# Queries and keys of the first block: projected by rows, turned in 16 columns a head, then transposed; the fifth conditioning chunk loaded ahead of the values'

## The reference, cut to what matters

```
c_act = silu(c)
mod   = c_act @ w_ada + b_ada                    # shift1, scale1, gate1, shift2, scale2, gate2
h     = rmsnorm(x) * norm_mix_g * (1 + scale1) + shift1
proj  = h @ w_in                                 # 512 pool | 512 q | 512 k | 512 v | 2048 gates
q, k  = rope_partial(q, pos), rope_partial(k, pos)   # 8 heads of 64
attn  = causal softmax attention over 256 tokens
merged = sigmoid(gates) * (pooled @ w_branch_pool) + ... attn @ w_branch_attn
x     = x + gate1 * (merged @ w_out)
x     = x + gate2 * peer_ffn(...)                # 256 rows of gathered experts a token tile
...then the second block: attention, convolution FFN

def rope_partial(x, pos):          # only 16 of a head's 64 columns turn
    x1, x2, rest = x[..., :8], x[..., 8:16], x[..., 16:]
    return concatenate([x1 * cos - x2 * sin, x1 * sin + x2 * cos, rest])
```

## Time and profile before

| | us |
|---|---|
| median of 3 runs | 1170.46 |
| lowest, highest | 1169.34, 1170.64 |
| the profiled execution | 1169.51 |
| its span in the profile | 1167.7 |
| its mean granted TensorE clock | 0.976 of full speed |

### The profile page before, as it was taken

The page is one execution under the profiler, slowest core; times in us unless marked ns, Lnnn a source line. Parts: engine busy times, 40 slices in busy tenths (PEclk is TensorE's granted clock), DMA queues, the critical chain, the costliest instruction groups (busy, mean ns, idle before and its releaser), DMA issues.

```text
span 1167.7 us, 13710 instructions
## 1 busy us (share of the span) xinstructions
PE 1037.7 (89%) x5050; PEld 698.5 (60%) x5050; DVE 824.5 (71%) x1912; ACT 420.8 (36%) x895; POOL 301.0 (26%) x262
## 2 busy tenths in 40 slices
PE   6989999989999896887877788788899999999997
PEld 3889976645555443432323333233389878999986
DVE  6599765867777767788878655555566878888843
ACT  3545622322332132132221211111266666565631
POOL 0000001444554553444544444445000000000000
PEclk9999999999999999988988999989999999999999
DMA  9977593999999999999999999999894443554530
GB/s 377 424 322 299 236 403 153 422 421 421 421 421 420 421 421 421 421 409 421 421 422 422 421 422 421 422 421 422 340 393 180 145 181 144 191 208 170 192 144 36
DMA packets 48342, 390.44 MB, mean 334 GB/s; under 512 B 5514, under 2 KB 5906, under 8 KB 7316
## 3 DMA queue, kind: packets, MB, share of 16 engines
q0 software_dynamic: 37040, 269.51, 55.6%
q1 hardware_dynamic: 11236, 120.07, 26.3%
HBM read 388.50 MB, written 1.06 MB: 334 GB/s over the span
## 4 chain that ended last, share of the span: by engine, by line
PE 51%; DMA 34%; DVE 11%; ACT 2%; issue 2%; POOL 1%; SPq 0%; DVEq 0%
DMA ring<-in_uv,idx 30%; PE ps L1466 18%; PE ps L1832 13%; PE ps L1989 5%; DMA ring<-in_w_ada 3%; DVE ring L1252 3%; PE ps L1700 2%; PE ps L1642 2%; PE ps L1917 2%; PE ps L1490 1%; DVE ring L904 1%; DVE ring_r L893 1%; PE ps L1715 1%; PE ps L1519 1%; ACT probT L765 1%
## 5 line engine op out<-in xcount | busy, mean ns | idle before, releaser
L1832 PE MATMUL ps<-ring,probT 128*128 128x512 f32 x1020 | 490.1, 624 | 102.0 <-ACT probT L765 101.9
L1252 DVE CUSTOM_DVE_ANT_0 ring<-h2t,ring 128x1024 f32<-128x1024 f32 x255 | 309.9, 1223 | 178.6 <-DMA ring<-in_uv,idx 178.3
L1832 PEld LDWEIGHTS ps<-ring,probT 128*128 128x128 f32 x1020 | 190.8, 198 | 337.7 <-issue 189.9
L522 POOL DMA_INDIRECT ring<-in_uv,idx x255 | 298.6, 1171 | 325.8 <-PE ps L1832 275.7
L1466 PE MATMUL ps<-util_r,ring_r 128*128 128x256 f32 x1216 | 204.6, 282 | 0.0
L893 DVE TENSOR_TENSOR ring_r<-ring,ring_r 128x1024 fp32r<-128x1024 f32 (+1 forms) x134 | 155.6, 1205 | 36.3 <-ACT ring_r L544 36.3
L1466 PEld LDWEIGHTS ps<-util_r,ring_r 128*128 128x128 f32 x1216 | 169.7, 188 | 0.8 <-issue 0.7
L760 ACT ACTIVATE prob<-prob 128x2 f32<-128x2 f32 (+2 forms) x98 | 20.0, 204 | 400.7 <-DVE prob L1252 400.5
L544 ACT ACTIVATE ring_r<-ring 128x1024 fp32r<-128x1024 f32 (+1 forms) x134 | 131.9, 1039 | 44.4 <-DMA ring<-in_w_in 22.0
L1466 PE MATMUL ps<-h_r,ring_r 128*128 128x256 f32 x704 | 125.2, 281 | 0.6 <-DVE util_r L1224 0.6
L765 ACT ACTIVATE probT<-ct,prob 128x128 f32<-128x128 f32 x256 | 85.5, 392 | 87.0 <-DVE prob L1258 86.4
(11 more groups left out here) (217 smaller groups left out, 995.5 us busy)
## 6 DMA issues: line engine op xcount, KB each, us to landing
ring<-in_w_in SPq DMA_DIRECT2D x11, 2048.0 KB, 12.4
ring<-in_w_up SPq DMA_DIRECT2D x11, 2048.0 KB, 7.9
ring<-in_w_ada SPq DMA_DIRECT2D x7, 2048.0 KB, 10.0
ring<-in_w_down SPq DMA_DIRECT2D x6, 2048.0 KB, 7.9
ring<-in_w_ada SPq DMA_DIRECT2D x8, 1024.0 KB, 14.1
ring<-in_w_out SPq DMA_DIRECT2D x4, 2048.0 KB, 9.5
ring<-in_w_q SPq DMA_DIRECT2D x3, 2048.0 KB, 11.6
ring<-in_w_in SPq DMA_DIRECT2D x4, 1024.0 KB, 10.3
```

Of the source, the lines that this page charges most:

```text
L522: e.indirect_dma_start(out=row_buf[n], out_offset=None, in_=uv, in_offset=bass.IndirectOffsetOnAxis(ap=idx[:, tt, k:k + 1], axis=0)).then_inc(
L1252: e.tensor_tensor_reduce(u, h2t[:, tt, :], u, 1.0, 0.0, ALU.mult, ALU.add, av[:, tt, n % 128:n % 128 + 1]).then_inc(*made.put(("dot", n)))
L1832: ins = e.matmul(acc[half][:, :], diag[:, n % 8, :], row_buf[n][:, D + half * 512:D + (half + 1) * 512], start=(k == 0), stop=(k == 127))
```

## The change

Three edits.

1. Queries (`in 1`) and keys (`in 2`) are projected by rows, as the values were. ScalarE copies each token tile's 128 x 512 result into rows (`rows_of`), for queries in the area of `yT`, for keys in `small`. VectorE turns only the 16 columns of each head in place, for all 8 heads and both tiles at once: two products of 128 x 256 elements into `turning`, a difference and a sum of 128 x 128 elements. TensorE transposes the rows in 128 x 128 pieces, 16 a name, into two groups, and ScalarE copies these to `qT` and `kT`.
2. The constants `rot`, `cosm`, `sinm` (640 columns) give way to `cosr`, `sinr` (64 columns). The second constants' load falls from 1024 to 448 columns, from 512 to 224 KB.
3. The order: `ada 4` loads ahead of `in 3`; VectorE's order is `split_low(4..11), rope("q"), ada(4) pieces 0 to 2, split_low(12, 13), ada(4) piece 3, rope("k"), split_low(14, 15), ada(6), split_low(16, 17), ada(5), split_low(18, 19)`. TensorE transposes queries behind all four quarters of the keys, and keys between the values' halves.

```
-             ("in", 3, 3), ("ada", 4, 1), ("ada", 6, 4), ...
+             ("ada", 4, 1), ("in", 3, 3), ("ada", 6, 4), ...
...scalar
+            def projected_rows(name, scale=1.0):
+                i, _ = head_of_rope[name]
+                for tt in range(2):
+                    act.wait_ge(done, ("tokens", i, tt))
+                    e.activation(rows_of[name][:, tt, :], bank(("tokens", i, tt))[:, :], ACT.Copy, scale=scale)...
+            def columns_of_rows(name):
+                _, x3 = head_of_rope[name]
+                for j0 in (0, 2):
+                    act.wait_ge(done, ("turned rope", name, j0))
+                    e.activation(x3[:, j0:j0 + 2, :], pair(("turned rope", name, j0)), ACT.Copy)...
+            projected_rows("q", -0.125)
+            split_high(12, 13)
+            columns_of_rows("q")
+            projected_rows("k")
+            split_high(14, 15)
             split_high(16, 17)
+            columns_of_rows("k")
...vector
+                for tt in range(2):
+                    dve.wait_ge(acted, ("v", i, tt))
+                for dst, table in ((by_cos, "cosr"), (by_sin, "sinr")):
+                    e.tensor_tensor(dst, x[:, :, :, 0:16], <table over heads>, ALU.mult)...
+                e.tensor_tensor(x[:, :, :, 0:8], by_cos[:, :, :, 0:8], by_sin[:, :, :, 8:16], ALU.subtract)...
+                e.tensor_tensor(x[:, :, :, 8:16], by_cos[:, :, :, 8:16], by_sin[:, :, :, 0:8], ALU.add)...
...tensor
+            def turned_rope(name):
+                pe.wait_ge(made, ("roped", name))
+                for j0 in (0, 2):
+                    o = group(("turned rope", name, j0))
+                    for jj in range(2):
+                        for tt in range(2):
+                            ins = e.transpose(o[:, jj * T + tt * P:jj * T + (tt + 1) * P],
+                                              rows_of[name][:, tt, (j0 + jj) * P:(j0 + jj + 1) * P], ident)
-            columns("in", 2, 0, ...); rope("q"); columns("in", 2, 2, ...)
-            tokens("in", 3, 0, ...); rope("k"); tokens("in", 3, 2, ...)
+            tokens("in", 2, 0, ...); tokens("in", 2, 2, ...); turned_rope("q")
+            tokens("in", 3, 0, ...); turned_rope("k"); tokens("in", 3, 2, ...)
             columns("in", 4, 0, ...)
```

More of the change, by code:

```diff
@@ L30 @@
 KF = FF // P
-CONST = dict(ident=128, ones=128, iota=16, eps=1, eps5=1, one=1, rot=128, cmask=384, cosm=256, sinm=256)
+CONST = dict(ident=128, ones=128, iota=16, eps=1, eps5=1, one=1, cmask=384, cosr=32, sinr=32)
 COLS = dict(b_ada=48, g_mix=8, pscale=4, g_ffn=8, g_fin=8, ln1g=8, ln1b=8, ln2g=8, ln2b=8,
@@ L312, in build @@
         merged = three(util, 4096, 8)
-        rope_of = {"q": (qT, yT), "k": (kT, small[:, :].rearrange("p (j t) -> p j t", j=4))}
+        rows_of = {"q": A3[:, 4].rearrange("p j t -> p (j t)").rearrange("p (s n) -> p s n", s=2),
+                   "k": small[:, :].rearrange("p (s n) -> p s n", s=2)}
+        head_of_rope = {"q": (1, qT), "k": ("k", kT)}
+        turning = [probT[:, z, 0:256].rearrange("p (s h d) -> p s h d", s=2, h=8) for z in range(2)]
         Q3 = area[:, 0:4096].rearrange("p (j t) -> p j t", j=16)
@@ L1039, in vector @@
             split_low(*range(4, 12))
-            ada(4)
+            rope("q")
+            ada(4, (0, 1, 2))
             split_low(12, 13)
-            rope("q")
+            ada(4, (3,))
+            rope("k")
             split_low(14, 15)
@@ L1047, in vector @@
             split_low(18, 19)
-            rope("k")
             def modulation2():
@@ L1583, in tensor, with first_half @@
             xs = hi_r, lo_r
[L1584 to L1589, removed]
+            first = {i: [group(("tokens", i, tt)) for tt in range(2)] for i in (0, 1)}
+            def first_half(i, k0):
+                w = slots[SLOT_OF["in", i]].rearrange("p (k n) -> p k n", k=KD)
                 for tt in range(2):
@@ L1593, in mixer_half @@
                         pe.wait_ge(acted, ("modulated", k))
-                        ins = e.matmul(mixer[tt][:, :], h_sb[:, k, tile[tt]], w[:, k, :], start=(k == 0), stop=(k == KD - 1))
+                        ins = e.matmul(first[i][tt][:, :], h_sb[:, k, tile[tt]], w[:, k, :], start=(k == 0),
+                                       stop=(i == 0 and k == KD - 1))
                     if k0 == 4:
-                        ins.then_inc(*done.put(("tokens", 0, tt)))
+                        ins.then_inc(*done.put(("tokens", i, tt)))
@@ L1598, in tensor @@
             pe.wait_ge(half_loaded["in", 0], ("in", 0))
-            mixer_half(0)
+            first_half(0, 0)
             pe.wait_ge(half_loaded["in", 1], ("in", 1))
[L1601 to L1604, removed]
+            first_half(1, 0)
             pe.wait_ge(loaded[SLOT_OF["in", 0]], ("in", 0))
-            mixer_half(4)
+            first_half(0, 4)
@@ L1612, in tensor @@
                 wait_low(q)
[L1613 to L1620, removed]
@@ L1621, in tensor @@
-            pe.wait_ge(acted, unit("in", 1, 2))
-            rope("q")
-            columns("in", 2, 2, xs, lambda k: [], acted)
+                wait_low(q + 1)
+                for tt in range(2):
+                    o = first[1][tt][:, z * P:(z + 2) * P].rearrange("p (q n) -> p q n", q=2)
+                    for k in range(4, KD):
+                        pe.wait_ge(made, ("x low", 1, k))
+                        for n, (w, r) in enumerate(((wh, xs[0]), (wh, xs[1]), (wl, xs[0]))):
+                            ins = e.matmul(o, r[:, k, tt * P:(tt + 1) * P], w[:, k - 4, :, :], start=False,
+                                           stop=(z == 2 and k == KD - 1 and n == 2))
+                    ins.then_inc(*done.put(("quarter", q + tt) if z == 0 else ("tokens", 1, tt)))
@@ L1624, in tensor @@
+            for tt in range(2):
+                banks.give(("tokens", 1, tt), acted, ("v", 1, tt))
+            tokens("in", 2, 0, xs, lambda k: [])
+            tokens("in", 2, 2, xs, lambda k: [])
+            turned_rope("q")
             tokens("in", 3, 0, xs, lambda k: [])
-            pe.wait_ge(acted, unit("in", 2, 0))
-            pe.wait_ge(acted, unit("in", 2, 2))
-            rope("k")
+            turned_rope("k")
             tokens("in", 3, 2, xs, lambda k: [])
             columns("in", 4, 0, xs, lambda k: [], acted)
-            pe.wait_ge(made, ("roped", "q", 0))
@@ L2047, in constants @@
     ang = s.astype(np.float32)[:, None] * inv.astype(np.float32)[None, :]
[L2048 to L2058, removed]
+    for name, table in (("cosr", np.cos(ang)), ("sinr", np.sin(ang))):
+        put(name, np.concatenate([table, table], 1).reshape(2, P, 16).transpose(1, 0, 2).reshape(P, 32))
     put("iota", np.arange(16)[None, :])
```

72 lines of the change are left out of this document (36 added, 36 removed).

## The result

| | before | after | ratio, 95% interval |
|---|---|---|---|
| first chip, 6 runs each | 1170.28 | 1165.32 | 0.9957 (0.9946 to 0.9967) |
| second chip, 5 after and 17 before | 1169.31 | 1166.12 | 0.9966 (0.9952 to 0.9979) |
| third chip, 5 after and 9 before | 1170.02 | 1164.54 | 0.9954 (0.9940 to 0.9968) |

The kernel became faster by 5.0, 3.2 and 5.5 us. The forecast was 3.6. The profiled execution of the changed kernel took 1165.48 us, with a span of 1163.7.

A forecast was written before the change was run, and what follows sets the result against it. Bound: the experts' row stream, whose start hangs on TensorE's first scores. 4.24 of stalls less 0.37 transposes less 0.27 passes gives 3.6 us: 1170.46 to 1166.9; likeliest case 1165.5 to 1168.1, range 1165.3 to 1170.0.

The forecast's parts named there:

- Added are 32 transposes: TensorE's rotation: 32 transposes at 0.11 us, 3.52 us, replace 16 matmul records of 3.15 us, 0.37 more than before.
- The form of the passes: TensorE's projections by rows: four blocks at 5.68 to 5.80 us each; 0.27 us subtracted from the gain.
- The stalls: TensorE's four pauses ahead of the scores, 1.13, 1.52, 0.12 and 1.47 us, together 4.24, would go.
- VectorE's rotation: 12 wide operations give way to 8 small ones at 0.36 us; VectorE is freed of 5.3 us.
- The wait for two quarters at once: TensorE wants quarters 8 and 9 low at 48.37 us; ready at 48.27, just fits; bound 0 to 0.6 lost.
- The new wait: VectorE stands still from 59.9 to 63.6 us before the keys' rotation; costs TensorE nothing, margins 0.4 to 2.7 us.
- The loads: `ada 4` lands at 49.6 us instead of 55.30, `in 3` at 54.6; SyncE's waits are no worse.
- After the scores: VectorE has room, entering 3.9 us or more earlier; tightest load `out 1` keeps 3.3 us of room.
- the stall that reaches TensorE: Rival, chance 0.14: VectorE's stall delays TensorE, 2 us of the 3.6 lost, time 1168.9 us.
- The gain taken back before the gathers: Rival, chance 0.08: unmoved loads lose all but 0.7 us of the earlier landings, time 1169.8 us.
- Transposes at full price: Rival, chance 0.04: transposes don't overlap and cost 0.273 us each, sum 5.2 us worse, time 1172.1 us.
- a clock that falls for them: Rival, chance 0.06: transposes drop TensorE to 1.2 GHz; two blocks cost 11.4 us, time 1178 us.

The follow-up runs named there:

- e_order_old: Changed kernel with old order of loads and VectorE's work, keys' transposes directly ahead of the scores: 1174.17 us, ratio 1.0035 to the kernel before the change.

## Why the prediction was wrong

*The step that failed* is "Added are 32 transposes", in the part on TensorE's rotation. There are 16: two groups of two columns of blocks by two token tiles are 8 a name, and the forecast counted 16 a name, as does the description of the change ahead of it. The change's code shows it, and the rows x8 of the profile after. The price was right: 0.11 was taken, 0.099 to 0.108 measured. So the term is 1.58 us and not 3.52, and instead of costing 0.37 more than the 3.15 of the matrix, the transposes save 1.57. With the count right and all else as written, 16 x 0.11 = 1.76, the scores would be forecast at 78.8 and the time at 1165.1. The run with 16 a name moved the scores by 1.7 us and the one with 64 by 12, so this term is on the path to the scores in full.

*The form of the passes*: taken as midway between 5.68 and 5.80 a block. The four blocks took 5.60, 5.60, 5.70 and 5.69, together 22.6 us against the 22.96 midway: 0.4 us better, and a little below the lower bound, 22.72. The upper bound was drawn from one block. (The sum's 0.27 for this term should be 0.24 by its own bounds.)

With these the sum closes: 4.24 of stalls, 1.57 of transposes and 0.13 of the form, less 0.08 each for a gates' block of 5.76 and a start at 48.45 instead of 48.37, is 5.78 us, what the scores gained. The two errors went the same way. The likeliest case's lower end took the transposes as dear as the matrix, so it held only 0.4 of the 1.9 us of the count; it comes to 1165.6 by its own terms and was written as 1165.5, and nothing is given for the step to 1165.3. That the time fell just outside and not just inside is chance; the count isn't.

*The stalls* (4.24 us): right. All four are gone. *VectorE's rotation*: 1.22 us a name, 1.43 taken. *The wait for two quarters at once*: right that it exists and that smaller constants take it away. That it had room was luck: the chunk came 1.9 us earlier and not 0.7, so quarter 9 was low at 47.06, 1.4 us ahead and not 0.1. With the old constants the wait is 0.96 us, where 0 to 0.6 was given. *The new wait*: right in place and size (3.4 us, 3.7 worked out) and in costing nothing, as the runs with 1.79 and 0.92 us of it show. *The loads*: right that nothing stands in their way, but the order of the loads needed no credit. *After the scores*: "it had room" was nearly right of VectorE, but the forecast looked only at VectorE and the loads and not at ScalarE. From scores to first gather the changed kernel loses 0.4 to 0.7 us, mostly at ScalarE: the chunk that landed at 76.72 moved by 0.8 us and not by 5.8, and holds the values' copies, the table load and the exponentials behind four high halves. Its row stood in the earlier trace rows and was followed no farther than its landing. The tightest load that the forecast named, `out 1`, was never waited for: TensorE's row of line 1732 at 157.91 us runs through without a pause.

*The rivals*: the stall that reaches TensorE appears only if the rotation is made wide again, and then costs 2.4 us, where 2.0 was worked out from the changed kernel's margins. The gain taken back before the gathers is real at 0.4 to 0.7 us, not at 3. Transposes at full price and a clock that falls for them are excluded by the run with 128 of them. The rival that decides on the other side, a lower clock, did appear in this stretch, between 60 and 68 us, but behind a pause of TensorE and only in the experiment that brought the pause.

*What stays open*: 0.4 to 0.9 us in the gather stage, and the spread of the gain, 3.2 to 5.5 us, over three chips. Part of it is seen in single executions. The first two profiles differ by 5.8 us at the scores, 5.4 at the first gather, 4.9 behind the gathers and 4.0 at the end, and the last 0.9 is a lower clock that came in some executions of either kernel (below).

## What to carry to other kernels

Count an added instruction by its loops, written out, before pricing it; a price good to 10% was spoiled here by a count wrong by a factor of two. When narrow work frees an engine, look for where its programs place it: the same operations gained 3.2 to 5.5 us in one order and lost 4.6 in another. When an edit of an earlier stage pays only in part, read the chain that ended last again: here half of what the scores moved was taken up behind them. And when a stage is moved forward, list the waits in it that end with something that doesn't move, a landing above all, and follow each to the engine that stands behind it.

## What the runs showed of the hardware

After a pause of 2.96 us that ended at 62.71 us (`e_order_old`), TensorE was granted 0.91 of full speed between 60 and 64 us and 0.67 between 64 and 68; from 64 to 66 alone it was 0.50, its 1.2 GHz level. After pauses of 1.36 and 1.76 us near 69 us, in the two profiles of the kernel before, and of 1.78 us near 84 us in `e_order_old`, it stayed at 1.00. Behind a pause of 2.05 us between two groups of 16 transposes, which ended at 971.56 us in the kernel before and at 966.66 in the changed one, it fell in some executions and not in others. Stretch 964 to 974 us of the kernel before in its two profiles, granted clock third from the right:

```profile
964.00:974.00 10.00, 7.56 (x48) 6.24 (x46) 8.86 (x19) 4.99 (x10) 0.00 (x0) 1.00 0.53 203
```

```profile
964.00:974.00 10.00, 7.95 (x44) 6.91 (x43) 7.98 (x16) 4.64 (x9) 0.00 (x0) 0.85 0.57 211
```

In the second it was 0.50 from 972 to 974 us, the lower level again. The changed kernel's three profiles have 0.83, 0.83 and 1.00 from 964 to 974. From the transposes behind the pause to the end of the convolution's first 22 blocks it took 127.85 us in the two profiles with 1.00, one of each kernel, and 128.71, 128.73 and 128.94 in the three others. So the lower clock costs 0.9 to 1.1 us, and it came in either kernel.

The keys' chunk landed 2.1 us later when 288 KB more stood ahead of it (45.62 against 43.53), and the chunks behind it 0.8 later, about what those bytes take at 426 GB/s (0.7). One landing thus moved by more than the bytes ahead of it take; what shifts it here wasn't found.
